# A hybrid RG-LRU and attention block: the stacked neighbour rows of the gate tiles copied by ScalarE and VectorE, and the first gate tile stacked as well

## The chip, the core and the metric

The kernel runs on one core of one Trainium2 chip. The metric is the device time of one execution in microseconds, the median of several runs. TensorE multiplies, VectorE, ScalarE and POOL (GpSimd) work element by element, SP (SyncE) issues transfers, and so can ScalarE's queue.

## What is computed

One layer of an encoder over 1024 frames of width 1024, in float32. Only its recurrent branch matters here:

```python
u = conv(u) + conv_b                                   # depthwise, 4 taps, 1280 channels
ub = u.reshape(B, S, N_LRU_BLOCKS, LRU_BLOCK)          # 16 blocks of 80 channels
r = jax.nn.sigmoid(jnp.einsum("bsnc,ncd->bsnd", ub, w_rg).reshape(B, S, D_RNN) + b_rg)
i = jax.nn.sigmoid(jnp.einsum("bsnc,ncd->bsnd", ub, w_ig).reshape(B, S, D_RNN) + b_ig)
log_a = -LRU_C * r.astype(jnp.float32) * jax.nn.softplus(-lru_lambda.astype(jnp.float32))
a = jnp.exp(log_a)
b = jnp.sqrt(-jnp.expm1(2.0 * log_a)) * (i * u).astype(jnp.float32)
_, h = lax.associative_scan(_lru_combine, (a, b), axis=1)
```

The rest (windowed attention, merge of the branches, SwiGLU) is large, and the change doesn't touch it.

## The kernel before

Frames are worked on in two halves of 512 (`h` = 0, 1); channels lie on the 128 partitions. Each float32 product is made of three matmuls over operands that are split in a high and a low part: high x high, high x low, low x high. Weights are loaded by SP into a ring of four blocks `w_raw` and split by POOL into `w_hi` and `w_lo`. A load is issued when the block that was in its place is split, and a block is split when TensorE is done with the one before it in its place (`blocks_done`).

**Gate tiles.** The 1280 channels make ten tiles of 128, `j` = 0 to 9, but the gates' blocks have 80 channels, so a tile's gates need its own channels and some of a neighbour tile. Of tiles 1, 2, 3, 6, 7, 8 (`MIXED`) the needed rows of both neighbours together fill one operand of 128 partitions, `mix_hi` and `mix_lo`, in slot `j % 3`. Tiles 4, 5 and 9 (`NEAR`) need only 32 rows of one neighbour. Theirs are stacked: partitions 0 to 31 of `mix_hi` hold the high part, 32 to 63 the low part, 64 to 95 the high part again, with weights stacked to match, and one matmul over 96 partitions does what three do elsewhere. Tile 0 needs 16 channels of tile 1; it reads tile 1's `uc_hi` and `uc_lo` whole, with three matmuls. So a gate has six matmuls in tiles 0 to 3 and 6 to 8, and four in tiles 4, 5 and 9; each tile has two gates (r and i).

**A step.** `recurrent` on TensorE runs steps `j` = 2 to 9. In each: `project(0)`, 24 matmuls, makes the conv's input of tile `j`; then `gates(j - 2)`, 12 or 8 matmuls; then `project(2)`, 24 matmuls, the GeLU branch. So in this text step 6 makes the gates of tile 4, step 7 those of tile 5, step 8 those of tile 6. The gates of tiles 8 and 9 follow in `kvq`.

ScalarE in step `j`, in this order: `conv_in` (L1369 to L1378, which waits for `project(0)`), the rounding of an output (L1435), the gates' functions of tile `j - 2` (tanh L1403 and L1405, exp L1410, tanh L1412, which wait for the gates), `conv_hi` (L1383: the high part `uc_hi` of tile `j`), `gate_root` (a table load and a sqrt, L1418), `mix` (the transfers L1390 and L1395, which wait for `uc_lo`), `decay` (L1430, waits for VectorE) and the GeLU (a table load and L1424). VectorE in step `j`: three taps of the conv (L1927), L1963, the low part `uc_lo` (L1933, behind `uc_hi`), and the recurrence of tile `j - 2` (L1939 to L1957).

**The transfers.** `mix(j)` copies, from partition to partition, rows of tile `j` into the operands of its neighbours `j - 1` and `j + 1`: one transfer of 256 KB into each mixed one (L1390), three of 64 KB into a stacked one (L1395). They are issued on ScalarE's queue. A mixed tile `j` is complete with the transfer from tile `j + 1`, in step `j + 1`, and its gates follow in step `j + 2`. TensorE waits for them in `gates`, ahead of the tile's first matmul; the trace gives that wait at L915.

## Time and profile before

| | |
|---|---|
| median of 3 runs | 1620.09 us |
| lowest, highest | 1619.33, 1626.31 us |
| profiled execution, device time | 1621.06 us |
| its span, first to last instruction | 1619.2 us |
| instructions | 24286 |
| granted TensorE clock, mean | 0.997 of full speed |
| VectorE busy | 905.0 us (56%) |
| ScalarE busy | 572.3 us (35%) |
| POOL busy | 1234.4 us (76%) |
| DMA | 188.86 MB, mean 117 GB/s |

Times of the profile count from the first instruction of the span. Busy time of TensorE overlaps (a matmul of 512 columns is shown with 0.39 us, and the next one starts 0.23 us behind its start), so its stream is read by starts. PE is TensorE's matmul, PEld its weight load, DVE VectorE, ACT ScalarE; a name with q is that engine's sequencer or queue. Brackets behind a row give the engine's idle time before it and what ended it.

### The profile page before, as it was taken

The numbers are of one execution on the slowest core, as the hardware profiler recorded it, in microseconds if no ns is written. First come the engines' busy times: TensorE is split into PE (matmuls) and PEld (weight loads), VectorE is DVE, ScalarE is ACT, GpSimd is POOL, SyncE is SP. The second block draws the span as 40 slices with busy tenths as digits, with TensorE's granted clock in tenths as the row PEclk, the third lists the DMA queues.
The fourth block names the chain that finished last, engine by engine and source line by source line (L and its number), as shares of the span: only waits on it lengthen the run. The fifth ranks groups of instructions, "written<-read, shape, count | busy, mean of one in ns | idle before, by whom it ended". The sixth has DMA issues, their size and how long they took to land.

```text
span 1619.2 us, 24286 instructions
## 1 busy us (share of the span) xinstructions
PE 1603.6 (99%) x7390; PEld 1327.0 (82%) x7390; DVE 905.0 (56%) x1158; ACT 572.3 (35%) x1078; POOL 1234.4 (76%) x1330
## 2 busy tenths in 40 slices
PE   9999999999999999999999999999999999999997
PEld 7888888888888888888888878888888888788887
DVE  6565646652165666676622579677865558405502
ACT  4787335532226885255422244100010013102100
POOL 5787866777777788777777777788887778877875
PEclk9999999999999999999999999999999999999999
DMA  5445432233344454522333583344422222733632
GB/s 165 131 120 131 132 91 80 74 101 93 97 144 128 121 133 114 166 77 74 92 97 95 150 286 107 97 118 117 119 75 75 65 65 69 245 93 114 222 107 87
DMA packets 121462, 188.86 MB, mean 117 GB/s; under 512 B 13668, under 2 KB 45796, under 8 KB 121380
## 3 DMA queue, kind: packets, MB, share of 16 engines
q1 hardware_dynamic: 97476, 144.03, 32.1%
q10 hardware_dynamic: 23904, 43.79, 8.2%
q8 instruction: 45, 0.74, 0.2%
q14 instruction: 37, 0.30, 0.1%
HBM read 162.73 MB, written 17.56 MB: 111 GB/s over the span
## 4 chain that ended last, share of the span: by engine, by line
PE 90%; DVE 4%; issue 2%; ACT 2%; ACTq 0%; DMA 0%; POOL 0%; DVEq 0%; SPq 0%; POOLq 0%
PE ps L872 14%; PE ps L871 14%; PE ps L870 14%; PE ps L1128 8%; PE ps L1127 8%; PE ps L1129 8%; PE ps L1225 4%; PE ps L1226 4%; PE ps L1227 4%; PE ps L950 1%; PE ps L946 1%; PE ps L947 1%; PE ps L1038 1%; DVE rows L2152 1%; DVE rows_r L2311 1%
## 5 line engine op out<-in xcount | busy, mean ns | idle before, releaser
L688 POOL TENSOR_TENSOR w_lo<-w_raw,w_hi 128x512 fp32r<-128x512 f32 (+2 forms) x374 | 448.3, 1199 | 31.2
L685 POOL TENSOR_SCALAR w_hi<-w_raw 128x512 fp32r<-128x512 f32 (+2 forms) x374 | 242.5, 648 | 194.4 <-PE ps L872 127.3
L872 PE MATMUL ps<-h_hi,w_lo 128*128 128x512 f32 x672 | 263.8, 393 | 0.0
L871 PE MATMUL ps<-h_lo,w_hi 128*128 128x512 f32 x672 | 263.6, 392 | 0.0
L870 PE MATMUL ps<-h_hi,w_hi 128*128 128x512 f32 x672 | 262.1, 390 | 0.7 <-DVE g_h L1950 0.6
L870 PEld LDWEIGHTS ps<-h_hi,w_hi 128*128 128x128 f32 x672 | 126.2, 188 | 28.9 <-DVE g_h L1950 1.5
L871 PEld LDWEIGHTS ps<-h_lo,w_hi 128*128 128x128 f32 x672 | 126.2, 188 | 27.5
L872 PEld LDWEIGHTS ps<-h_hi,w_lo 128*128 128x128 f32 x672 | 126.3, 188 | 26.1
L1127 PE MATMUL ps<-t,w_hi 128*128 128x512 f32 x352 | 138.2, 392 | 0.6 <-POOL w_lo L763 0.5
L1128 PE MATMUL ps<-t,w_hi 128*128 128x512 f32 x352 | 138.7, 394 | 0.0
L1129 PE MATMUL ps<-t,w_lo 128*128 128x512 f32 x352 | 136.6, 388 | 0.0
L1894 DVE TENSOR_TENSOR acc<-acc,sq 128x512 f32<-128x512 f32 x31 | 33.7, 1088 | 146.4 <-ACT sq L1620 134.2
L717 POOL TENSOR_SCALAR w_hi<-w_raw 128x512 fp32r<-128x512 f32 (+1 forms) x100 | 65.3, 653 | 45.5 <-PE ps L872 40.5
L730 POOL TENSOR_TENSOR w_lo<-w_raw,w_hi 128x512 fp32r<-128x512 f32 x72 | 93.8, 1303 | 6.0
L763 POOL TENSOR_TENSOR w_lo<-w_raw,w_hi 128x512 fp32r<-128x512 f32 x60 | 87.0, 1451 | 5.0
L1717 ACT ACTIVATE rstd_a<-rstd_a 128x512 f32<-128x512 f32 x22 | 13.9, 632 | 194.9 <-DVE rstd_a L2298 194.9
L1127 PEld LDWEIGHTS ps<-t,w_hi 128*128 128x128 f32 x352 | 66.1, 188 | 16.8 <-issue 1.4
L1129 PEld LDWEIGHTS ps<-t,w_lo 128*128 128x128 f32 x352 | 66.1, 188 | 14.8
L1128 PEld LDWEIGHTS ps<-t,w_hi 128*128 128x128 f32 x352 | 66.2, 188 | 13.1
L2119 DVE SCALAR_TENSOR_TENSOR tmp<-tmp,ps 128x512 f32<-128x512 f32 x16 | 11.0, 688 | 114.0 <-PE ps L872 114.0
L1620 ACT ACTIVATE sq<-ps 128x512 f32<-128x512 f32 (+1 forms) x15 | 9.0, 598 | 178.8 <-PE ps L1227 174.7
L1539 ACT ACTIVATE prob<-prob,stat 128x128 f32<-128x128 f32 x128 | 49.7, 389 | 63.3 <-DVE stat L2048 63.3
(389 smaller groups left out, 4105.7 us busy)
## 6 DMA issues: line engine op xcount, KB each, us to landing
w_raw<-w_f SPq DMA_DIRECT2D x68, 256.0 KB, 3.2
w_raw<-w_step SPq DMA_DIRECT2D x64, 256.0 KB, 2.8
w_raw<-w_b SPq DMA_DIRECT2D x64, 256.0 KB, 3.1
w_raw<-w_d SPq DMA_DIRECT2D x64, 256.0 KB, 2.7
w_raw<-w_a SPq DMA_DIRECT2D x96, 128.0 KB, 2.1
w_raw<-w_q SPq DMA_DIRECT2D x32, 256.0 KB, 3.1
w_raw<-w_o SPq DMA_DIRECT2D x32, 256.0 KB, 3.1
mix_hl<-uc_hl ACTq DMA_DIRECT2D x24, 256.0 KB, 4.7
```

Source lines behind the costliest of these rows:

```text
L685: nc.gpsimd.tensor_scalar(w_hi[:, s, w], w_raw[:, s, w], 1.0, 0.0, ALU.mult, ALU.add).then_inc(w_hi_made, 1)
L688: nc.gpsimd.tensor_tensor(w_lo[:, s, w], w_raw[:, s, w], rd(w_hi[:, s, w]), ALU.subtract).then_inc(w_lo_made, 1)
L717: nc.gpsimd.tensor_scalar(w_hi[:, s, w], w_raw[:, s, w], 1.0, 0.0, ALU.mult, ALU.add).then_inc(w_hi_made, 1)
L730: nc.gpsimd.tensor_tensor(w_lo[:, s, w], w_raw[:, s, w], rd(w_hi[:, s, w]), ALU.subtract).then_inc(w_lo_made, 1)
L763: nc.gpsimd.tensor_tensor(w_lo[:, s, :], src, rd(w_hi[:, s, :]), ALU.subtract)\
L870: mm(out, w_hi[:, s, w], x_hi, start=(k == 0), stop=False)
L871: mm(out, w_hi[:, s, w], x_lo, start=False, stop=False)
L872: last = mm(out, w_lo[:, s, w], x_hi, start=False, stop=(k == total - 1))
L1127: mm(ps[:, bank, :], w_hi[:, slot, w], x_hi[:, k, :], start=(q == 0), stop=False)
L1128: mm(ps[:, bank, :], w_hi[:, slot, w], x_lo[:, k, :], start=False, stop=False)
L1129: last = mm(ps[:, bank, :], w_lo[:, slot, w], x_hi[:, k, :], start=False, stop=(q == K2 - 1))
L1225: mm(out, w_hi[:, s, w], hi(k), start=(k == 0), stop=False)
```

## The change

The three transfers into each stacked tile go. Instead ScalarE, right behind `uc_hi` of the neighbour tile, copies 32 rows of it to partitions 0 to 31 and 64 to 95 of the operand, and VectorE, behind `uc_lo`, subtracts the same 32 rows (conv result less `uc_hi`) into partitions 32 to 63. These copies move data between partitions, for tile 4 from tile 3, for tile 5 from tile 6, for tile 9 from tile 8. Tile 0 joins the stacked tiles, with rows 0 to 31 of tile 1: its gates have four matmuls each in place of six, SP loads its weights with two transfers per block, one of which repeats 32 rows three times, and POOL splits them as for the other stacked tiles. TensorE waits on two new semaphores for the stacked tiles, and on `mix_made` for the mixed ones alone.

```diff
-NEAR = {4: (3, P - 32), 5: (6, 0), 9: (8, P - 32)}
-STACK = ((0, 0), (32, 1), (64, 0))
+NEAR = {0: (1, 0), 4: (3, P - 32), 5: (6, 0), 9: (8, P - 32)}
+NEAR_LIST = list(NEAR)
 STACKED = 96
 
 def mix_count(h, j):
-    same = range(j % 3, KR, 3)
-    dmas = [2 if i in MIXED else len(STACK) if i in NEAR else 0 for i in same]
-    return 16 * (h * sum(dmas) + sum(dmas[:j // 3 + 1]))
+    same = [i for i in MIXED if i % 3 == j % 3]
+    return 32 * (h * len(same) + same.index(j) + 1)
+
+def near_count(h, j):
+    return len(NEAR) * h + NEAR_LIST.index(j) + 1
...
+        def near_of(j):
+            return [(to, slice(r, r + 32)) for to, (of, r) in NEAR.items() if of == j]
...
-                    elif i not in NEAR:
-                        sp_eng.dma_start(w_raw[:, s, 0:2 * P], dram[g, :, off:off + 2 * P])\
-                            .then_inc(w_loaded[s], 16)
                     else:
-                        own = off + P
+                        own = off + (P if i else 0)
...
-                    if size < 4 and i:
+                    if size < 4:
                         used[s] += 2 if i in MIXED else 1
...
-                if j:
+                if j in MIXED:
                     pe.wait_ge(mix_made[j % 3], mix_count(h, j))
+                else:
+                    pe.wait_ge(near_hi_made, 2 * near_count(h, j))
+                    pe.wait_ge(near_lo_made, near_count(h, j))
...
                     if j not in NEAR:
-                        near_hi, near_lo = ((mix_hi[:, j % 3, :], mix_lo[:, j % 3, :]) if j else
-                                            (uc_hi[:, 1, :], uc_lo[:, 1, :]))
+                        near_hi, near_lo = mix_hi[:, j % 3, :], mix_lo[:, j % 3, :]
...
             def conv_hi(h, j, q):
                 act.wait_ge(taps, (j + KR * h) * 3 + 3)
                 fn(uc_hi[:, q, :], uc_of(q), ACT.Copy).then_inc(uc_hi_made, 1)
+                for to, r in near_of(j):
+                    act.wait_ge(uc_hi_made, j + KR * h + 1)
+                    for row in (0, 64):
+                        fn(mix_hi[row:row + 32, to % 3, :], rd(uc_hi[r, q, :]), ACT.Copy)\
+                            .then_inc(near_hi_made, 1)
...
-                    elif to in NEAR and NEAR[to][0] == j:
-                        r = slice(NEAR[to][1], NEAR[to][1] + 32)
-                        for row, part in STACK:
-                            act.dma_start(rd(mix_hi[row:row + 32, to % 3, :]), rd(uc_hl[r, part, j % 4, :]))\
-                                .then_inc(mix_made[to % 3], 16)
...
                 tt(uc_lo[:, q, :], uc_of(q), rd(uc_hi[:, q, :]), ALU.subtract)\
                     .then_inc(uc_lo_made, 1)
+                for to, r in near_of(j):
+                    tt(mix_hi[32:64, to % 3, :], uc_of(q)[r, :], rd(uc_hi[r, q, :]), ALU.subtract)\
+                        .then_inc(near_lo_made, 1)
```

## Rows read from the trace of the kernel before

**Rows 1.** Part 1 of the page: busy time, share of the span, number of instructions.

```profile
PE 1603.6 (99%) x7390; PEld 1327.0 (82%) x7390; DVE 905.0 (56%) x1158; ACT 572.3 (35%) x1078; POOL 1234.4 (76%) x1330
```

**Rows 2.** Timeline of TensorE, tiles 0, 5, 1 (second half): start, length, instruction.

```profile
45.14 0.39 PE L917 MATMUL ps<-uc_hl,w_hi 128*128 128x512 f32 x1
...
47.89 0.39 PE L870 MATMUL ps<-h_hi,w_hi 128*128 128x512 f32 x1
...
112.93 0.39 PE L917 MATMUL ps<-uc_hl,w_hi 128*128 128x512 f32 x1
...
114.78 0.40 PE L870 MATMUL ps<-h_hi,w_hi 128*128 128x512 f32 x1
...
518.73 0.39 PE L917 MATMUL ps<-uc_hl,w_hi 128*128 128x512 f32 x1
```

**Rows 3.** Timeline of TensorE at the start of tile 6's gates.

```profile
125.55 0.40 PE L872 MATMUL ps<-h_hi,w_lo 128*128 128x512 f32 x1
...
125.97 0.47 PE L917 MATMUL ps<-uc_hl,w_hi 128*128 128x512 f32 x1
...
126.28 0.40 PE L918 MATMUL ps<-uc_hl,w_hi 128*128 128x512 f32 x1
```

**Rows 4.** TensorE's waits at L915 (length in ns): tiles 6, 1 (second half), 2.

```profile
L915 PEldq EVENT_SEMAPHORE  x1: 4231/4231/4231, 121.7 to 121.7; - x1
...
L915 PEldq EVENT_SEMAPHORE  x1: 3316/3316/3316, 514.6 to 514.6; - x1
...
L915 PEldq EVENT_SEMAPHORE  x1: 3764/3764/3764, 68.5 to 68.5; - x1
```

**Rows 5.** Timeline of ScalarE in steps 6 and 7.

```profile
106.42 0.57 ACT L1383 ACTIVATE uc_hl<-ps 128x512 fp32r<-128x512 f32 x1
...
110.64 0.63 ACT L1430 ACTIVATE g_a<-g_r 128x512 f32<-128x512 f32 x1 [1.70 <-DVE g_s L1943]
...
112.58 0.60 ACT L1424 ACTIVATE gy<-ps 128x512 f32<-128x512 f32 x1
...
113.23 0.20 ACT L1369 ACTIVATE u_raw<-u_carry 128x3 f32<-128x3 f32 x1
...
114.76 0.62 ACT L1435 ACTIVATE lru_hi<-g_h 128x512 fp32r<-128x512 f32 x1
...
115.29 0.67 ACT L1403 ACTIVATE g_r<-ps,half_b 128x512 f32<-128x512 f32 x1
...
120.60 0.65 ACTq L1390 DMA_DIRECT2D mix_hl<-uc_hl  x1
```

**Rows 6.** Timeline of ScalarE in step 4.

```profile
72.91 0.20 ACT L1369 ACTIVATE u_raw<-u_carry 128x3 f32<-128x3 f32 x1 [0.39 <-PE ps L872]
...
75.64 0.69 ACT L1403 ACTIVATE g_r<-ps,half_b 128x512 f32<-128x512 f32 x1 [0.58 <-PE ps L925]
```

**Rows 7.** Timeline of POOL, ScalarE and VectorE around tile 0, first and second half.

```profile
39.97 0.41 POOL L717 TENSOR_SCALAR w_hi<-w_raw 128x256 fp32r<-128x256 f32 x1 [1.52 <-PE ps L950]
...
41.58 0.60 ACT L1383 ACTIVATE uc_hl<-ps 128x512 fp32r<-128x512 f32 x1 [2.49 <-DVE ps L1927]
...
510.56 2.25 DVE L1927 SCALAR_TENSOR_TENSOR ps<-u_raw,par,ps 128x512 f32<-128x512 f32 x3
```

**Rows 8.** Timeline of VectorE in step 6.

```profile
109.05 0.69 DVE L1942 SCALAR_TENSOR_TENSOR g_r<-g_a,g_r 128x512 f32<-128x512 f32 x1 [0.73 <-ACT g_s L1418]
...
109.66 0.95 DVE L1943 SCALAR_TENSOR_TENSOR g_s<-g_a,g_s 128x512 f32<-128x512 f32 x1
```

**Rows 9.** Instructions of L1933 and L1943: count, ns min/median/max.

```profile
L1933 DVE TENSOR_TENSOR uc_hl<-ps,uc_hl x20: 691/692/693, 34.2 to 607.4; 128x512 fp32r<-128x512 f32 x20
...
L1943 DVE SCALAR_TENSOR_TENSOR g_s<-g_a,g_s x20: 677/680/1784, 55.8 to 636.8; 128x512 f32<-128x512 f32 x20
```

**Rows 10.** Instructions of L1544 and L1539 between 244 and 245 us.

```profile
L1544 ACTq FUSED_REGOPS  x1: 43/43/43, 244.6 to 244.6; - x1
...
L1539 ACT ACTIVATE prob<-prob,stat x4: 385/386/387, 243.8 to 245.0; 128x128 f32<-128x128 f32 x4
```

More of the change, by code:

```diff
@@ L399, in build @@
             sem("a_made"), sem("gelu_made"), sem("lru_hi_made"))
+        near_hi_made, near_lo_made = sem("near_hi_made"), sem("near_lo_made")
         iu_made, loss_made, amp_made, b_made, scanned, h_kept, lru_made, lru_lo_made = (
@@ L545, in load_gates @@
                                          .rearrange("(o r) c -> o r c", o=1)
-                                         .broadcast_to([len(STACK), 32, P])).then_inc(mix_loaded[s], 16)
+                                         .broadcast_to([STACKED // 32, 32, P])).then_inc(mix_loaded[s], 16)
                         sp_eng.dma_start(w_raw[:, s, 0:P], dram[g, :, own:own + P])\
```

## The prediction

> **What bounds the kernel now.** Part 1 of the page comes first: TensorE's matmuls are busy for 99% of the span [rows 1]. So time can only be had by giving TensorE less to do or by closing a gap in its stream, and it can only be lost by opening one. The change touches the gate tiles, so I next read TensorE's timeline there. A tile with three near-matmuls per gate takes from 45.14 to 47.89, 2.75 us for twelve matmuls; a stacked tile takes from 112.93 to 114.78, 1.85 us for eight [rows 2]. Both run at one pace, 0.23 us from start to start.
>
> The third view is TensorE's own wait ahead of a gate tile. The wait for the transfers that fill `mix_hl` ended at 121.7 + 4.23 = 125.9 for tile 6, and the first matmul began at 125.97, 0.42 us behind the one before it, and the next 0.31 us later [rows 3, 4]. Against the pace of 0.23 that is (0.42 - 0.23) + (0.31 - 0.23) = 0.27 us lost. So the transfers of the mixed tiles land just in time, and the list of idle times, which sees hardly any of this because matmul records overlap, would not have told it. Who is late at tile 6? ScalarE's timeline answers: from 113.23, right behind the gelu that ends at 113.18, it works without a pause to the gates' tanh at 115.29, on to the exps and the copy `uc_hi`, and the transfer for tile 6 goes out at 120.60 [rows 5]. In the steps of full-length gates ScalarE does pause for TensorE: 0.39 us ahead of L1369, 0.58 us ahead of L1403 [rows 6]. Tile 6 is different since the gates of tile 5 ahead of it are the short, stacked ones: TensorE is through them 0.9 us sooner, ScalarE isn't.
>
> **The change part by part.**
>
> *Tile 0 stacked.* Two halves, each 2.75 - 1.85 = 0.90 us: 1.80 us off TensorE, if nothing is late next. Its stacked rows come from tile 1. In the first half the copy `uc_hi` of tile 1 starts at 41.58, two ScalarE copies follow and are through by about 43.4, and the gates start at 45.14: free [rows 2, 7]. POOL makes a tile-0 block by four short instructions in place of two; it had waited 1.52 us for TensorE ahead of this block and has made it by some 41.2, over 4 us before use: free [rows 7]. SP issues four loads for the two blocks in place of two; POOL's releaser there is TensorE, not a load: free. If that cover were gone each would cost its own length, about 0.5 us.
>
> *What is late next at tile 1.* With tile 0 shorter, TensorE reaches tile 1 0.90 us sooner. In the first half the transfer for tile 1 hangs on ScalarE's chain behind the gates of tile 0, so it moves along. In the second half it doesn't: the conv of tile 2 starts at 510.56 only, behind VectorE's reciprocal, which nothing here moves [rows 7]. TensorE's wait ended at 514.6 + 3.32 = 517.92 [rows 4]. The matmul was at 518.73 [rows 2]; it would come at 517.83. By tile 6, a matmul follows the end of its wait by 0.06 us and loses 0.08 more behind it: 517.92 + 0.14 - 517.83 = 0.23 us lost.
>
> *Transfers of tiles 4, 5, 9 removed.* 18 issues of some 0.6 us on ScalarE's queue and 18 transfers go. Nobody waited for them: those of tiles 4 and 9 are done a step before use, those of tile 5 in time. The ScalarE instruction behind them (L1430) waits for VectorE's L1943 anyway [rows 5]. Worth nothing; at most a loss of tile 6's kind, 0.27 us, goes at tile 7, should its transfer land sooner with none behind it.
>
> *Sixteen ScalarE copies of 32x512.* Rows of such a copy don't exist; a copy takes by its columns, so I take the 128x512 copy L1435: 0.62 us, and the next starts 0.52 us behind its start [rows 5]. The first must wait for the copy `uc_hi` to end. In step 6 (for tile 5): L1383 ends at 106.99, copy one 107.05, copy two 107.57 to 108.19. What stood right behind L1383 stands behind copy two: ScalarE is 108.19 - 106.99 = 1.20 us later. VectorE's L1942 waits for the sqrt behind it and moves by as much, from 109.05 to 110.25, and L1943 from 109.66 to 110.86 [rows 8]. L1943 took 0.95 us here and 0.68 us at its median [rows 9], so L1430 starts at 111.57 to 111.84 in place of 110.64. The gelu ends at 114.11 to 114.38 in place of 113.18. L1369 followed TensorE at 113.23, so it is now 0.85 to 1.12 us later, and from there to the transfer for tile 6 nothing is slack. Tile 6 already waits, so all of it is new wait: 2 x (0.85 to 1.12) = 1.70 to 2.24, middle 1.97 us. The copies for tiles 4 and 9 (steps 3 and 8) delay ScalarE as much, but the next step holds 0.39 + 0.58 us of pauses [rows 6] before it could reach the transfers for tiles 3 and 8: nothing. The lower bound is zero in step 7 too, if the 32-row copies were far shorter than any row; the upper is the delay in every step (a rival).
>
> *Do the copies hold back the transfer issued behind them?* In steps 3 and 8 the transfers for tiles 2 and 7, due at once, stand behind the new copies in ScalarE's program. They start when `uc_lo` is made, if the sequencer runs ahead of the engine. It does: at 244.60 the sequencer handles L1544, which stands behind nine exps in the program, while the engine begins the fourth [rows 10]. So the transfers still go out on time: nothing.
>
> *Eight VectorE subtractions* of 32x512, PSUM and SBUF in. The row alike is L1933: 0.691 to 0.693 us in all 20 [rows 9]. VectorE waits for the sqrt there (0.73 us idle ahead of L1942 [rows 8]) and has the time: nothing. The trace also shows L1943, two SBUF inputs, at 0.68 to 1.78 us [rows 9]. The Trainium skill ("SBUF — State Buffer", Who interferes with whom) has it that a VectorE instruction with two SBUF inputs is blocked by a GpSimd one that reads SBUF, and blocks it in turn. By that rule the new subtraction, one input from PSUM, stays at 0.69 us, and the trace's constant L1933 agrees; but L1942 and L1943 of step 6, moved by 1.2 us, may fall on another POOL instruction and take up to 1.1 us more or lose the 0.27 they now have too much, which would put tile 6 at 0.85 to 2.2 us per half.
>
> **Sum.** -1.80 + 0.23 + 1.97 = +0.40 us. The profiled execution took 1621.06 us (span 1619.2, 1.9 around it), which gives 1621.46; the median of the runs stands 0.97 below it: 1620.09 + 0.40 = 1620.5. Its own range is the sum's ends (+0.13 to +0.67) and half a microsecond per half for how long the tile 6 transfer takes when it starts later: 1619.3 to 1621.8.
>
> **The rivals.**
> (a) *The delay never reaches tile 6*, because the copies are short or the pauses take it up. Then -1.80 + 0.23 = -1.57: 1618.5. For it: ScalarE's queue loses 18 issues of 0.6 us. Against: those issues lie beside the engine's work, and the path from 113.18 on is closed. 0.27.
> (b) *Slower: the transfers for tiles 2 and 7 wait behind the copies.* Each goes out up to 1.2 us later. Tile 2's wait ended at 68.5 + 3.76 = 72.3 [rows 4]; its first matmul came at about 72.6, by L1369 at 72.91, which the matmul before it (0.39 us long) released [rows 6]. Less the 0.14 us from wait to matmul that is about 0.2 us of room. Priced for all four with that room: 4 x (1.2 - 0.2) = 4.0 us on the forecast, 1624.5. It decides from the point where the issue starts over 0.1 us behind the end of `uc_lo`. Against: [rows 10]. 0.10.
> (c) *The delay passes through steps 4 and 9 as well*, to tiles 3 and 8: four times 1 us, less their room, for which tile 2's 0.2 us stands: 3.2 us on the forecast, 1623.7. Against: the pauses [rows 6]. 0.08.
> (d) *The change doesn't do its work*: tile 0 is not shorter, since a stacked matmul contracts over fewer rows and not fewer columns. The timeline of tile 5 excludes it: same pace, fewer matmuls. 0.02.
>
> **How the numbers follow.** The forecast has 0.51, (a) 0.27, (b) 0.10, (c) 0.08, (d) and the rest 0.04. The range of 8 in 10 takes in the forecast, (a) with some tenths for the spread of the runs, and (c): 1618.2 to 1623.8. It leaves out (b) and the rest. A measurement of this kernel can tell about 0.5%, 8.1 us, from no change. No case reaches that; even 1.2 us in each of eight places comes to 9.6 - 1.8 = 7.8. So same 0.97, faster 0.01 and slower 0.02, for what isn't thought of.
>
> **What would show it.** Tile 0: from its first matmul to the next projection's 1.85 us, like tile 5, with eight matmuls. Tile 6: the two matmul intervals at its start sum to 1.1 to 1.4 us over pace in both halves, and ScalarE's tanh of tile 5's gates about 1 us later against TensorE. Tile 1 of the second half: 0.2 us over pace. L1390 in steps 3 and 8 still at the end of `uc_lo`; the table load in steps 3, 6 and 8 about 1.2 us behind the end of `uc_hi`. If tile 6 is no later than before, (a) holds and I took the copies too long or the path too tight; if L1390 starts late in steps 3 and 8, (b). The prediction is most exposed in the length of one transfer (5.3 us for tile 6) and in where VectorE meets POOL.

## The result, and the profile after

The changed kernel took 1624.3 us (median of 12; the kernel before 1620.8 us, median of 12 beside it). The ratio is 1.0023, with a 95% interval of 1.0015 to 1.003: the change costs 3.5 us by the medians and 0.23% by the ratio. That is less than the 0.5% below which the prediction calls two times the same, but the interval doesn't hold 1. One of the twelve executions took 1988.41 us at a granted clock of 0.752 and is left out of the ratio. The forecast was +0.4 us, 1620.5 us, and the time lies above the top of the range, 1623.8. The profiled execution took 1625.44 us with a span of 1623.6 us, 4.4 above that of before (1619.2), at a mean granted clock of 0.996.

Part 1 of the page after, beside [rows 1]: TensorE has eight matmuls fewer and is as busy as before, VectorE is 16 us busier (of which the eight subtractions are 5.5) and ScalarE 9.

```profile
PE 1603.8 (99%) x7382; PEld 1326.6 (82%) x7382; DVE 920.9 (57%) x1166; ACT 581.1 (36%) x1094; POOL 1239.7 (76%) x1338
```

What TensorE waited for, by line (total us, times, longest us); L925 is the first matmul of a gate tile, as L917 was before.

```profile
PE ps L925 <- issue: 3.9, 4, 1.3
...
PE ps L1045 <- DVE prob L2066: 1.3, 2, 1.0
...
PE ps L875 <- ACT gy L1431: 0.4, 1, 0.4
```

Four gate tiles wait now. The timeline of TensorE says which, and what has become of tile 0: tile 0 (first half, first matmul, and the next projection's), tile 6 (first half), tile 1 (second half), a projection in step 4 (second half), tile 3 (second half), and tile 6 (second half).

```profile
45.40 0.39 PE L925 MATMUL ps<-uc_hl,w_hi 128*128 128x512 f32 x1
...
47.26 0.40 PE L875 MATMUL ps<-h_hi,w_hi 128*128 128x512 f32 x1
...
126.72 0.47 PE L925 MATMUL ps<-uc_hl,w_hi 128*128 128x512 f32 x1 [1.32 <-issue]
127.03 0.39 PE L926 MATMUL ps<-uc_hl,w_hi 128*128 128x512 f32 x1
...
519.76 0.47 PE L925 MATMUL ps<-uc_hl,w_hi 128*128 128x512 f32 x1 [0.61 <-issue]
520.07 0.40 PE L926 MATMUL ps<-uc_hl,w_hi 128*128 128x512 f32 x1
...
536.10 0.39 PE L932 MATMUL ps<-mix_hl,w_lo 128*128 128x512 f32 x1
536.94 0.51 PE L875 MATMUL ps<-h_hi,w_hi 128*128 128x512 f32 x1 [0.45 <-ACT gy L1431]
...
549.00 0.47 PE L925 MATMUL ps<-uc_hl,w_hi 128*128 128x512 f32 x1 [0.78 <-issue]
549.31 0.40 PE L926 MATMUL ps<-uc_hl,w_hi 128*128 128x512 f32 x1
...
590.21 0.47 PE L925 MATMUL ps<-uc_hl,w_hi 128*128 128x512 f32 x1 [1.23 <-issue]
```

Tile 0 takes 47.26 - 45.40 = 1.86 us in place of 2.75, as forecast. The losses are counted as in the prediction, by the starts against a pace of 0.23 us; the profile's bracket is smaller than a start interval, since records overlap. Tile 6 loses 1.57 us in the first half (its first matmul starts 1.71 behind the one before it, the next 0.31 later) and 1.48 in the second, where it lost 0.27 and 0.33 before [rows 3]. Tile 1 of the second half loses 0.85, tile 3 of the second half 1.03, and the projection of step 4 in the second half 0.72 (intervals 0.84 and 0.34). Tile 7, which lost 0.15 before in the first half, loses nothing.

From the first matmul of tile 0 to that of tile 9, the two halves took 116.78 + 116.69 us before and 117.11 + 119.87 after: +3.51 us. This is the whole of the measured 3.5 to 3.7. The single entries make

| us, after less before | |
|---|---|
| tile 0, both halves | -1.80 |
| tile 1, second half | +0.85 |
| tile 6, 1.30 + 1.15 | +2.45 |
| step 4, second half: projection 0.72, tile 3 1.03 | +1.75 |
| tile 7 | -0.15 |
| sum | +3.10 |

and 0.4 us are left. Of these, 0.25 lie behind tile 3 of the second half: from 549.31 to 563.08 us TensorE's matmuls start 0.2333 us apart, and elsewhere in these steps 0.2289, at a granted clock of 1.00 in both. The rest of the span's 4.4 is a later start (0.26) and a wait of 0.52 at the start of the first half's attention (747 ns at 250.02, L1045), which the kernels below have or don't have without a pattern that could be tied to the change.

Now to ScalarE in steps 6 and 7, beside [rows 5].

```profile
105.84 0.57 ACT L1390 ACTIVATE uc_hl<-ps 128x512 fp32r<-128x512 f32 x1
106.44 1.29 ACT L1394 ACTIVATE mix_hl<-uc_hl 32x512 fp32r<-32x512 f32 x2
107.17 0.60 ACTq L1402 DMA_DIRECT2D mix_hl<-uc_hl  x1
107.75 1.28 ACT L1425 ACT_TABLE_LOAD   x1
...
111.53 0.63 ACT L1437 ACTIVATE g_a<-g_r 128x512 f32<-128x512 f32 x1 [1.85 <-DVE g_s L1953]
...
113.48 0.60 ACT L1431 ACTIVATE gy<-ps 128x512 f32<-128x512 f32 x1
...
116.02 0.67 ACT L1410 ACTIVATE g_r<-ps,half_b 128x512 f32<-128x512 f32 x1
...
121.33 0.61 ACTq L1402 DMA_DIRECT2D mix_hl<-uc_hl  x1
```

The copies (L1394) hold the engine from 106.41 to 107.75, 1.34 us, where 1.20 was forecast. `decay` (L1437) starts 5.12 us behind the end of `uc_hi` (106.41 to 111.53); before it was 110.64 - 106.99 = 3.65 [rows 5]. Of these 1.47 us, 1.32 come from the copies (L1952 below starts 3.38 us behind `uc_hi`, L1942 stood 2.06 behind it), and 0.15 is VectorE's, whose L1953 took 1.10 us and not 0.95 [rows 8]. From there to the transfer for tile 6 there are 121.33 - 111.53 = 9.80 us, before 9.96 [rows 5]: a closed path, as foreseen. ScalarE's tanh of tile 5's gates comes 3.67 us behind their first matmul (112.34 to 116.02), 2.36 before [rows 2, 5]: 1.3 us later, where about 1 was forecast. The third row is the one that bears on rival (b): the transfer for tile 7 goes out at 107.17, in the middle of the copies.

VectorE and POOL in the same step:

```profile
109.79 0.69 DVE L1952 SCALAR_TENSOR_TENSOR g_r<-g_a,g_r 128x512 f32<-128x512 f32 x1 [1.34 <-ACT g_s L1425]
110.40 1.10 DVE L1953 SCALAR_TENSOR_TENSOR g_s<-g_a,g_s 128x512 f32<-128x512 f32 x1
```

```profile
109.92 1.04 POOL L722 TENSOR_SCALAR w_hi<-w_raw 128x512 fp32r<-128x512 f32 x1 [0.33 <-PE ps L877]
```

And in step 3 of the second half, VectorE, then POOL, then ScalarE:

```profile
531.87 1.84 DVE L1952 SCALAR_TENSOR_TENSOR g_r<-g_a,g_r 128x512 f32<-128x512 f32 x1 [1.18 <-ACT g_s L1425]
```

```profile
531.86 1.29 POOL L735 TENSOR_TENSOR w_lo<-w_raw,w_hi 128x512 fp32r<-128x512 f32 x1
```

```profile
534.34 0.64 ACT L1437 ACTIVATE g_a<-g_r 128x512 f32<-128x512 f32 x1 [2.57 <-DVE g_s L1953]
...
536.29 0.60 ACT L1431 ACTIVATE gy<-ps 128x512 f32<-128x512 f32 x1
```

This is a row that the sum had no term for. VectorE's L1952, two SBUF inputs and 0.69 us long in most steps, starts 0.01 us behind POOL's L735 and takes 1.84 us. `decay` starts at 534.34, the GeLU ends at 536.89, the projection of step 4 starts at 536.94 on its release, and ScalarE, which begins step 4 this late, has no pause left before the transfer for tile 3.

The step was late before it came to its copies. In step 2 of the second half VectorE's two instructions take 1.09 and 1.78 us:

```profile
516.64 1.09 DVE L1952 SCALAR_TENSOR_TENSOR g_r<-g_a,g_r 128x512 f32<-128x512 f32 x1 [0.73 <-ACT g_s L1425]
517.65 1.78 DVE L1953 SCALAR_TENSOR_TENSOR g_s<-g_a,g_s 128x512 f32<-128x512 f32 x1
```

So step 3 begins late: `uc_lo` of tile 3 is made 529.24 - 519.76 = 9.48 us behind the first matmul of tile 1's gates, in the first half 8.37, and 8.35 in the kernel before. These 1.13 us come on top of the copies.

The three lines that the steps of the prediction spoke of (count, ns min/median/max):

```profile
L1394 ACT ACTIVATE mix_hl<-uc_hl x16: 627/630/637, 42.3 to 598.6; 32x512 fp32r<-32x512 f32 x16
```

```profile
L1943 DVE TENSOR_TENSOR mix_hl<-ps,uc_hl x8: 680/687/694, 43.0 to 598.7; 32x512 fp32r<-32x512 f32 x8
```

```profile
L1953 DVE SCALAR_TENSOR_TENSOR g_s<-g_a,g_s x20: 678/1099/1785, 54.8 to 641.1; 128x512 f32<-128x512 f32 x20
```

L1953 is the L1943 of before [rows 9]; its median went from 680 to 1099 ns. The new subtraction, one input in PSUM, is never stretched (694 ns at most).

### The profile page after: what moved, and what is told of

The parts are those of the page before. It is cut to its first block, busy times and chain, and to the rows that moved or that the text cites. A ratio compares the mean times of both kernels' runs of the same rounds, so it can differ in the third digit from the quotient of the medians.

```text
span 1623.6 us, 24296 instructions
## 1 busy us (share of the span) xinstructions
PE 1603.8 (99%) x7382; PEld 1326.6 (82%) x7382; DVE 920.9 (57%) x1166; ACT 581.1 (36%) x1094; POOL 1239.7 (76%) x1338
## 4 chain that ended last, share of the span: by engine, by line
PE 88%; DVE 5%; issue 3%; ACT 3%; DMA 1%; ACTq 0%; POOL 0%; DVEq 0%; SPq 0%; POOLq 0%
PE ps L877 14%; PE ps L876 14%; PE ps L875 13%; PE ps L1134 8%; PE ps L1136 8%; PE ps L1135 8%; PE ps L1232 4%; PE ps L1233 4%; PE ps L1234 4%; PE ps L953 1%; PE ps L957 1%; PE ps L954 1%; PE ps L1045 1%; DVE rows L2162 1%; DVE rows_r L2321 1%
## 5 line engine op out<-in xcount | busy, mean ns | idle before, releaser
L735 POOL TENSOR_TENSOR w_lo<-w_raw,w_hi 128x512 fp32r<-128x512 f32 x72 | 99.0, 1374 | 6.0
L768 POOL TENSOR_TENSOR w_lo<-w_raw,w_hi 128x512 fp32r<-128x512 f32 x60 | 87.1, 1451 | 5.0
```

The lines of the kernel that those rows point to most:

```text
L735: nc.gpsimd.tensor_tensor(w_lo[:, s, w], w_raw[:, s, w], rd(w_hi[:, s, w]), ALU.subtract).then_inc(w_lo_made, 1)
L768: nc.gpsimd.tensor_tensor(w_lo[:, s, :], src, rd(w_hi[:, s, :]), ALU.subtract)\
```

## The experiments

The theory: the copies make ScalarE late by their own length ahead of `decay`, in steps 6 and 3; at tile 6 this is lost at once, and in step 3 it is lost only where VectorE meets POOL as well. The rivals: the loss comes from tile 0's change and what it shifts; or it is mostly the meeting of VectorE and POOL, and the copies' length matters little. Ratios are against the kernel before on the same chip, with 95% intervals.

### The two halves of the change alone

`e1_tile0_only`: tile 0 stacked by copies, tiles 4, 5 and 9 by transfers as before.

```diff
-NEAR_LIST = list(NEAR)
+NEAR_LIST = [0]
+STACK = ((0, 0), (32, 1), (64, 0))
...
+                    elif to in NEAR and to not in NEAR_LIST and NEAR[to][0] == j:
+                        r = slice(NEAR[to][1], NEAR[to][1] + 32)
+                        for row, part in STACK:
+                            act.dma_start(rd(mix_hi[row:row + 32, to % 3, :]), rd(uc_hl[r, part, j % 4, :]))\
+                                .then_inc(mix_made[to % 3], 16)
```

> Tile 0 stacked by two ScalarE copies and one VectorE subtraction; tiles 4, 5 and 9 by transfers, as in the kernel before. My theory (the loss is ScalarE's delay by the copies in steps 3 and 6): tile 0 gives 2 x 0.90 = 1.80 us, tile 1 of the second half loses 0.85 us as in the changed kernel, tile 6 loses its old 0.3 us and no more, so 0.9 to 1.0 us faster than before, about 1619.8. Rival (a shorter tile 0 alone shifts the engines against each other and costs elsewhere): tile 3 of the second half or tile 6 lose a microsecond here too, and the time is equal to before or slower.

Measured: 1619.96 us, ratio 0.9996 (0.9984 to 1.0008). Tile 6 loses nothing in either half (its transfers took 4.92 and 4.91 us), tile 1 of the second half 0.86 us, tile 3 of the second half 0.10.

`e2_no_tile0`: tiles 4, 5 and 9 by copies, tile 0 as before.

```diff
-NEAR = {0: (1, 0), 4: (3, P - 32), 5: (6, 0), 9: (8, P - 32)}
+NEAR = {4: (3, P - 32), 5: (6, 0), 9: (8, P - 32)}
```

> Tiles 4, 5 and 9 by copies, tile 0 as before, unstacked. My theory: tile 6 loses 1.5 us in place of 0.3 in both halves (+2.4), tile 7 loses nothing in place of 0.15, so at least 2.2 us slower than before, about 1623.0; with the second half's VectorE wait in step 3 as well (+1.75), 1624.8. Rival (tile 0's change is the cause): no more than 0.5 us slower.

Measured: 1623.28 us, ratio 1.0016 (1.0005 to 1.0028). Tile 6 loses 1.78 and 1.23 us, no other tile anything. So the loss at tile 6 belongs to the copies, that at tile 1 of the second half to tile 0's stack. The two parts don't add up: by the medians -0.93 and +2.39 us against 1620.89 make +1.5, and both together cost 3.5. The entries of the traces say where the rest is: 1.75 us are those of step 4 in the second half, of which `e1_tile0_only` has 0.10 and `e2_no_tile0` nothing; and `e1_tile0_only` gains the 0.60 us that tile 6 lost before, which the whole change doesn't. (The traces' sums are -1.58 and +2.99; 0.68 of the latter is no wait but the slower pace of 0.2333 us, from 127 to 163 us.) Step 3 of `e2_no_tile0` in the second half says why. Two rows of VectorE in step 2, then one of VectorE and one of POOL in step 3:

```profile
516.66 0.69 DVE L1956 SCALAR_TENSOR_TENSOR g_r<-g_a,g_r 128x512 f32<-128x512 f32 x1 [0.73 <-ACT g_s L1429]
517.27 0.69 DVE L1957 SCALAR_TENSOR_TENSOR g_s<-g_a,g_s 128x512 f32<-128x512 f32 x1
```

```profile
530.88 0.69 DVE L1956 SCALAR_TENSOR_TENSOR g_r<-g_a,g_r 128x512 f32<-128x512 f32 x1 [1.18 <-ACT g_s L1429]
```

```profile
531.21 0.84 POOL L725 TENSOR_SCALAR w_hi<-w_raw 128x512 fp32r<-128x512 f32 x1 [1.50 <-PE ps L880]
```

Two things differ from the changed kernel. In step 2 nothing is stretched, and `uc_lo` of tile 3 is made 8.35 us behind the first matmul of tile 1, not 9.48. In step 3 the copies are there and L1956 is as late behind them, but it starts 0.33 us ahead of a POOL instruction and not just behind one; with L1957 the pair takes 1.79 us (0.69 and 1.10) and not 2.52 (1.84 and 0.68). The GeLU of step 3 ends 15.27 us behind the first matmul of tile 1, in the changed kernel 17.13: of these 1.86 us, 1.13 are brought along from step 2 and 0.73 arise in step 3. `e1_tile0_only` has the stretched step 2 as well (1.09 and 1.78 us, `uc_lo` at 9.48) but no copies in step 3, and loses 0.10. With tile 0 shorter, TensorE's stream, and with it POOL's, stands otherwise against VectorE's, in step 2 already. No run separates the 1.13 from the 0.73 beside the copies.

### The copies moved within the step

Copies can stand further back in ScalarE's program, behind the sqrt and the transfers, where ScalarE waits for VectorE anyway (1.85 us ahead of `decay` in the rows above). `e3_copies_late` does this in steps 3, 6 and 8.

```diff
+LATE = (3, 6, 8)
...
+                if j not in LATE:
+                    near_copies(h, j, q)
...
+                    if j in LATE:
+                        near_copies(h, j, j % 4)
```

> The changed kernel with ScalarE's copies of steps 3, 6 and 8 put behind the sqrt and the transfers, into ScalarE's idle time ahead of L1437; nothing else moved, VectorE's subtractions included. My theory: ScalarE's sqrt comes 1.3 us sooner again, tile 6 loses 0.3 us as in the kernel before, tile 3 of the second half nothing, tile 1 of the second half still 0.85 us: -1.80 + 0.85 = 0.95 us faster than before, about 1619.8. Rival (VectorE's eight subtractions, or transfers that land later because of what else changed, cost the time): tile 6 still loses 1 us or more and the time stays within 1 us of the changed kernel's 1624.3.

Measured: 1620.02 us, ratio 0.9992 (0.9981 to 1.0004); `e10_late_again` below, the same kernel, gives 1620.07. ScalarE in step 6, and TensorE at tile 6:

```profile
104.89 0.57 ACT L1391 ACTIVATE uc_hl<-ps 128x512 fp32r<-128x512 f32 x1
...
106.78 0.63 ACT L1430 ACTIVATE g_s<-g_r 128x512 f32<-128x512 f32 x1
107.31 1.27 ACT L1399 ACTIVATE mix_hl<-uc_hl 32x512 fp32r<-32x512 f32 x2
109.13 0.63 ACT L1442 ACTIVATE g_a<-g_r 128x512 f32<-128x512 f32 x1 [0.54 <-DVE g_s L1960]
```

```profile
124.00 0.39 PE L878 MATMUL ps<-h_hi,w_lo 128*128 128x512 f32 x1
124.23 0.39 PE L926 MATMUL ps<-uc_hl,w_hi 128*128 128x512 f32 x1
```

The same two copies stand in a pause of which 0.54 us is still left, `decay` starts 109.13 - 105.46 = 3.67 us behind `uc_hi` as before the change, and tile 6 starts in pace. The only loss of size is tile 1 of the second half, 1.18 us.

Three kernels move part of this. `e4_step6_late` has `LATE = (6,)`, `e5_step3_late` has `LATE = (3,)`, and `e7_one_copy` has step 6 alone and moves one of its two copies:

```diff
-                    for row in (0, 64):
+                    for row in rows:
...
+                near_copies(h, j, q, (0,) if j in LATE else (0, 64))
...
+                    if j in LATE:
+                        near_copies(h, j, j % 4, (64,))
```

> As the run with all copies put behind the sqrt, but only those of step 6 (for tile 5); steps 3 and 8 stay as in the changed kernel. My theory: tile 6's extra loss goes (2.4 us), the loss of step 3 in the second half (tile 3 and the projection ahead of it, 1.75 us) stays: about 1621.9. Rival (the delay of step 3 is what reaches tile 6): tile 6 still loses over 1 us and the time is above 1623.

> The changed kernel with ScalarE's copies of step 3 alone (for tile 4) put behind the sqrt; those of steps 6 and 8 stay ahead of it. My theory (two separate losses): the loss in the second half at the projection of step 4 and at tile 3 (0.7 + 1.0 us) goes, the loss at tile 6 (1.5 us in each half) stays: about 1622.5. Rival (one lag that begins in step 3 and is passed on to tile 6): tile 6 loses under 0.6 us too, and the time is about 1620.

> The changed kernel with one of step 6's two copies put behind the sqrt, the other left ahead of it: half the delay. My theory (tile 6 waits for all that ScalarE is late): tile 6 loses 0.85 to 1.0 us in place of 1.5 in each half, about 1623.1. Rival (the loss comes by a collision of VectorE and POOL that either occurs or doesn't): tile 6 loses either 0.3 or 1.5 us.

Measured (losses in us over pace, ' for the second half):

| | median us | ratio, interval | tile 6, 6' | tile 1' | step 4', tile 3' |
|---|---|---|---|---|---|
| changed kernel | 1624.3 | 1.0023, 1.0015 to 1.003 | 1.57, 1.48 | 0.85 | 0.72, 1.03 |
| step 3 late | 1622.49 | 1.0013, 1.0004 to 1.0022 | 0.97, 1.35 | 0.98 | none |
| one copy of step 6 late | 1622.22 | 1.0011, 1.0002 to 1.002 | 0.19, 0.70 | 1.06 | 0.48, 0.74 |
| step 6 late | 1621.26 | 1.0005, 0.9994 to 1.0016 | none, 0.27 | 0.96 | 0.57, 0.69 |
| steps 3, 6, 8 late | 1620.02 | 0.9992, 0.9981 to 1.0004 | none | 1.18 | none |

The copies lose time in two separate places: those of step 6 at tile 6, and those of step 3 at step 4 and tile 3. `e5_step3_late` came out as expected, `e4_step6_late` 0.6 us sooner, `e7_one_copy` 0.9 us sooner than its 1623.1.

The loss at tile 6 has two terms, and only one is the copies'. In the eight halves with both copies ahead of `decay` (the changed kernel, `e2`, `e5`, `e8` below) the transfer goes out 8.99 to 9.01 us behind the first matmul of tile 5, and the loss is its length less 3.7 us: 4.70 us long, it loses 0.97; 5.30 long, 1.57; 5.50 long, 1.78. In the kernel before it goes out at 7.68, and 5.28 us of length lose 0.27. So the copies are worth 1.3 us per half at equal length, and the spread of the length as much as 0.8.

The one copy left ahead of `decay` in `e7_one_copy` made the tanh of tile 5's gates 0.52 us late in the first half and 1.16 in the second. The difference is VectorE's and POOL's order. In the first half both start at 109.41, VectorE's L1958 1 ns behind POOL's L710, and POOL's is the one that is stretched (1.01 us, VectorE 0.69). In the second half VectorE is 10 ns behind POOL, and it is VectorE's:

```profile
571.02 1.00 DVE L1958 SCALAR_TENSOR_TENSOR g_r<-g_a,g_r 128x512 f32<-128x512 f32 x1 [0.68 <-ACT g_s L1429]
```

```profile
571.01 0.46 POOL L710 TENSOR_TENSOR w_lo<-w_raw,w_hi 128x128 fp32r<-128x128 f32 x1
```

So neither expectation of `e7_one_copy` held alone: half the copies and a meeting that occurs or doesn't both count.

In the kernel with step 6 late, tile 7 of the first half lost 0.62 us in turn: its transfer took 5.80 us, in the changed kernel 3.16. In that kernel step 3 is as in the changed one, and VectorE and POOL meet once more, this time at the second of the two instructions:

```profile
531.27 1.79 DVE L1960 SCALAR_TENSOR_TENSOR g_s<-g_a,g_s 128x512 f32<-128x512 f32 x1
```

```profile
530.76 1.74 POOL L736 TENSOR_TENSOR w_lo<-w_raw,w_hi 128x512 fp32r<-128x512 f32 x1
```

### Is it the copies or the meeting with POOL?

`m2_after_memset` is the changed kernel with POOL's splits of the weights that take 128x512 in the recurrent stage, and in the stages ahead and behind, replaced by memsets, which read nothing: the products with those weights are left out. `m1_before_memset` is the same in the kernel before.

```diff
-                        nc.gpsimd.tensor_scalar(w_hi[:, s, w], w_raw[:, s, w], 1.0, 0.0,
-                                                ALU.mult, ALU.add).then_inc(w_hi_made, 1)
+                        if size == 4:
+                            nc.gpsimd.memset(rd(w_hi[:, s, 0:2 * P]), 0.0)
+                            nc.gpsimd.memset(rd(w_hi[:, s, 2 * P:4 * P]), 0.0).then_inc(w_hi_made, 1)
...
+                        for part in range(8):
+                            last = nc.gpsimd.memset(rd(w_lo[:, s, 64 * part:64 * part + 64]), 0.0)
```

> The kernel before, with POOL's two instructions for each 128x512 weight block of the head, step and tail stages replaced by memsets of about the same length (two of 256 columns, eight of 64), which write and don't read; so these weights are zero and the projections of these stages leave their products out. Loads, waits and order stay. My theory (VectorE's instructions with two SBUF inputs wait for a POOL instruction that reads SBUF): in steps 2 to 9 no L1942 or L1943 takes over 0.75 us, other than beside the 128x256 and stacked blocks that stay; the time is within 1 us of the kernel before. Rival (the stretched lengths have to do with when VectorE starts against ScalarE): they stay stretched beside the memsets.

> The changed kernel with the same memsets in POOL, and the same products left out. My theory: VectorE's L1952 at 1.84 us and L1953 at 1.10 us in the steps with copies go back to 0.69 us; the second half's loss of 1.7 us behind step 3 goes or falls to under 0.5 us, tile 6 still loses by the copies alone, 1.0 to 1.3 us in each half. So against the same kernel without the change 0.5 to 1.5 us slower in place of 3.5. Rival (the collisions are a by-product, the copies alone do it all): tile 3 of the second half still loses 1 us and the difference stays 3 us or more.

Measured: 1619.63 us, ratio 0.9993 (0.9984 to 1.0001), for the kernel before, whose gate tiles lose nothing more (0.05 us in all); 1619.46, ratio 0.9989 (0.998 to 0.9997), for the changed one, which loses only 0.65 us at tile 1 of the second half and nothing at tile 6. One row of VectorE in step 6 of the latter, and the transfers of its mixed tiles (the last line gives the time to landing):

```profile
109.81 0.68 DVE L1958 SCALAR_TENSOR_TENSOR g_s<-g_a,g_s 128x512 f32<-128x512 f32 x1
```

```profile
L1407 ACTq DMA_DIRECT2D mix_hl<-uc_hl x24: 597/603/693, 34.6 to 606.6; - x24
...
DMA to landing us min/median/max: 3.1/3.3/5.0
```

`m1_before_memset` came out as expected. `m2_after_memset` didn't: at tile 6, 1.0 to 1.3 us of loss were expected in each half, and 0.5 to 1.5 us of time over `m1_before_memset`. But the run does two things at once, and its time is no proof of either side. The stretch is gone in step 6: the tanh of tile 5's gates came 3.26 us behind their first matmul, in the changed kernel 3.67 and before 2.36. So the copies alone make ScalarE 0.90 us late here and the meeting with POOL adds 0.41. But the memsets are also shorter than the splits (0.76 us for the second in place of 1.30), the loads go out earlier, and the transfer for tile 6 landed in 3.67 us where it took 5.30 in the changed kernel and 5.28 before. It landed 0.59 us ahead of tile 6's first matmul, so tile 6 would have been in time even with the 0.41. In the second half the stretch of step 2 is gone too (0.69 and 0.68 us), `uc_lo` of tile 3 is made at 8.43 and not 9.48, and tile 3 loses nothing. What the pair shows is the share of the meeting in the delay, and that tile 6 hangs on its transfer's length as much as on ScalarE.

### What stands behind tile 1 of the second half

Its transfer waits for the conv of tile 2, which waits for VectorE. Ahead of that conv VectorE sets a sum (`open_sum`) and four blocks of `kd` to zero. `e6_late_memsets` is `e3_copies_late` with all five memsets behind `uc_lo` of tile 2, `e8_after_memsets` the same in the changed kernel, and `e9_best` is `e3_copies_late` with the four of `kd` alone, at the end of the recurrent stage; `e10_late_again` is `e3_copies_late` once more, as its partner.

The edit of `e6_late_memsets`:

```diff
-                open_sum(1 + 2 * h)
-
-                for kd in (kd_hi, kd_lo):
-                    for half in range(2):
-                        r = slice(64 * half, 64 * half + 64)
-                        nc.vector.memset(rd(kd[r, :, 1 - half, :]), 0.0).then_inc(kd_zeroed, 1)
...
+                    if j == 2:
+                        open_sum(1 + 2 * h)
+                        for kd in (kd_hi, kd_lo):
+                            ...
```

> All ScalarE copies of steps 3, 6, 8 behind the sqrt, and VectorE's memsets behind tile 2's low part: both known losses taken away. My theory: total loss at the gate tiles under 0.5 us, so nearly the whole 1.80 us of tile 0 and the 0.8 us that the kernel before loses at its gates: 1.5 to 2.3 us faster than before, about 1619.0. Rival (the gain is capped by something behind the gates, as the end of the recurrence or the attention): the gates lose nothing, and still no faster than the 1620.0 of the kernel with late copies alone.

> The changed kernel, with VectorE's memsets (1.8 us) moved from ahead of tile 2's conv to behind its low part, nothing else. My theory (tile 1 of the second half waits since the conv of tile 2 is late there, and its step's lateness starts the loss of step 3): the transfer for tile 1 goes out at least 0.4 us sooner, tile 1 loses 0 to 0.45 us in place of 0.85, and the second half's loss behind step 3 (1.75 us) goes or shrinks, since without tile 0's change it did not occur: about 1621.7 to 1622.5. Rival (tile 3's loss comes from step 3's copies alone): only tile 1's part goes, about 1623.5.

> The kernel with ScalarE's late copies, and VectorE's four memsets of the key tiles moved from ahead of tile 2's conv to the end of the recurrent stage; the memset of the sum stays. My theory: the conv of tile 2 starts 1.3 us sooner, tile 1 of the second half loses under 0.5 us in place of 1.2; if the last attention chunk isn't hit by the collision that cost the kernel with all memsets late 1.4 us, 1.3 to 2.0 us faster than before, about 1619. Rival (tile 1's loss is the transfer's length, not its start): it still loses 0.8 us or more, and the time equals the one with late copies alone.

> The kernel with late copies once more, for a narrower interval: 0.5 to 1.3 us faster than before by the trace's sum (gates 1.3 us shorter, first attention chunk 0.5 us longer). Rival (no gain at all; the first measurement was luck): ratio 1.0000 or above.

Measured: `e6` 1620.46 us (0.9996, 0.9986 to 1.0006), `e8` 1625.62 (1.0032, 1.002 to 1.0044), `e9` 1618.74 (0.9994, 0.9981 to 1.0006), `e10` 1620.07 (0.9994, 0.9985 to 1.0004). In all three kernels with the memsets moved, the loss at tile 1 of the second half is gone: its transfer goes out 7.35 us (`e6`, `e8`) and 7.80 us (`e9`) behind the first matmul of tile 0 and not 9.20. So that wait was VectorE's. Yet only `e9` has a lower median than its like without the move, and the interval of its ratio holds 1. `e6` missed its 1619.0, and `e8` missed its 1621.7 to 1622.5 by over 3 us: it was expected that the loss behind step 3 of the second half would go or shrink with the one at tile 1, and tile 3 still loses 1.03 us. In `e8` tile 3 of the first half, in time in the changed kernel, loses 0.91 us as well. In both halves step 3 begins 0.48 us late (`uc_lo` at 8.83, since VectorE's step 2 has the memsets in it), and VectorE's two instructions then take 1.00 or 1.01 and 1.78 us beside the copies: the same three terms as in the changed kernel, each of another size.

The stages behind the first attention of the second half took 6.7 us more in the profiled execution of `e8` than in the changed kernel's (930.4 against 923.7). A wait of 1.26 us for VectorE at 808.39 is part of it. The rest is no wait. The same stretch of both, first `e8`, then the changed kernel (window, its length, then busy us and number of instructions of PE, PEld, DVE, ACT and POOL; granted clock, share and GB/s of the DMA):

```profile
1055.00:1350.00 295.00, 294.52 (x1262) 238.27 (x1262) 188.43 (x236) 29.65 (x48) 235.43 (x216) 1.00 0.31 87
```

```profile
1055.00:1350.00 295.00, 294.53 (x1287) 241.36 (x1286) 196.95 (x243) 29.66 (x48) 240.28 (x219) 1.00 0.32 87
```

TensorE is busy for all but 0.5 us in both, but `e8` gets through 25 matmuls fewer: they start 0.2333 us apart and not 0.2289, some 5.5 us in all, at a granted clock of 1.00 in both. No line of the edit acts there, and this execution took 1630.23 us, 4.6 above the median of its kernel. So it is taken here for this execution's, not the edit's; what sets the pace isn't known. Why the median of `e8` stands above the changed kernel's isn't shown: its gate stages are 0.90 us shorter, and the wait at 808.39 takes that back.

In `e6` the gate tiles lose 0.50 us in all, less than in `e3` (1.30), and the time isn't shorter. VectorE and POOL in the last attention stage, first `e6`, then `e3`:

```profile
801.50 1.75 DVE L2088 TENSOR_TENSOR q_lo<-rstd_a,q_hi 128x512 fp32r<-128x512 f32 x1 [1.30 <-ACT q_hi L1574]
```

```profile
801.41 1.30 POOL L694 TENSOR_TENSOR w_lo<-w_raw,w_hi 128x512 fp32r<-128x512 f32 x1
```

```profile
801.05 0.73 DVE L2088 TENSOR_TENSOR q_lo<-rstd_a,q_hi 128x512 fp32r<-128x512 f32 x1 [0.92 <-ACT q_hi L1574]
```

```profile
801.33 1.61 POOL L694 TENSOR_TENSOR w_lo<-w_raw,w_hi 128x512 fp32r<-128x512 f32 x1
```

In `e6` VectorE starts 0.09 us behind POOL and takes 1.75 us; TensorE then waits for it (1.29 us at 804.56). In `e3` VectorE starts 0.28 us ahead, takes 0.73, POOL's instruction takes 1.61 in place of 1.30, and TensorE doesn't wait there. What was won in one stage is given back in another by the order of two instructions 0.3 us apart.

## Why the prediction was wrong

*Tile 0, -1.80.* Right: 1.86 us per tile, and nothing of POOL's, SP's or ScalarE's added work ahead of it is late (`e1_tile0_only`).

*Tile 1 of the second half, +0.23; it was +0.85.* The mechanism was right, the size wrong. The issue stands where it was foreseen: 9.20 us behind the first matmul of tile 0 (506.14 to 515.34), before 9.21. But the step took the transfer's 3.7 us over from the trace of before, and it took 4.33. Before, the load that SP issues stood at 514.84, behind the transfer at 514.20; now it stands at 515.10, ahead of the transfer at 515.34. Counted from tile 0's first matmul the load goes out at 8.96 us and not 9.85: TensorE, 0.9 us earlier, frees the weight block earlier. The two halves of the change agree: 4.33 us in `e1_tile0_only`, with a load 0.24 ahead, 3.67 in `e2_no_tile0`, with one 0.65 behind.

*Tile 6, +1.97; it was +2.45.* The path is the one described, and this wait is the largest entry. Two terms were mis-sized, and ScalarE is 1.3 us late where 0.85 to 1.12 was forecast (114.11 and 114.38 less 113.23, the prediction's own figures, are 0.88 and 1.15). The copies were priced by a 128x512 copy that overlaps the next by 0.10 us; they are as long (0.63) but leave a gap of 0.03, so two hold the engine for 1.34 us and not 1.20. And L1953 was to take between 0.68 and 0.95 us; it took 1.10. The transfer's length, the third term, happened to be nearly the same as before (5.30 and 5.19 us against 5.28 and 5.33); that was luck, as the 4.70 to 5.50 us of the other kernels show. The sentence on the meeting with POOL had allowed for this, up to 2.2 us a half, but the sum and the range's ends took in only the gentle half of it.

*The copies of steps 3 and 8, nothing; they cost +1.75.* This is the step that failed: the pauses of 0.39 + 0.58 us [rows 6] were to take up the whole delay. They don't, not even where nothing is lost. Here is ScalarE at the start of step 4 of the first half, where 0.39 us of idle time stood before:

```profile
73.45 0.20 ACT L1376 ACTIVATE u_raw<-u_carry 128x3 f32<-128x3 f32 x1
```

The pause ahead of L1410 is gone as well, and the transfers for tiles 3 and 8 go out 8.85 us behind the first matmul of the tile ahead, before 8.37 to 8.46. So 0.4 to 0.5 us get through, as rival (c) had it, and cost nothing because these transfers had 0.33 to 0.74 us of room before and have 0.34 to 0.79 now. In the second half of the changed kernel this cover isn't enough, since two more delays come to the copies' 1.34 us: 1.13 from VectorE's meeting with POOL in step 2, which goes back to tile 0's change, and 0.73 more of VectorE in step 3 than in `e2_no_tile0`. Rival (c) described the path, priced at 3.2 us for four places; the loss came in one. The prediction reasoned on the two VectorE instructions in step 6 alone, where a row of the trace had shown L1943 at 1.78 us somewhere [rows 9], and it took tile 0's part and the copies' part as independent.

The Trainium skill ("SBUF — State Buffer", Who interferes with whom) has it that a VectorE instruction with two SBUF inputs contends with a GpSimd one that reads SBUF, not with one that only writes it, and that "Issue order, not op shape, decides who blocks." The traces agree: L1952 stretched to 1.84 us by a POOL instruction of 1.29 us that started 0.01 us ahead of it, POOL's L694 stretched from 1.30 to 1.61 us where VectorE was ahead, 0.68 us for L1958 beside memsets, and 680 to 694 ns for the subtraction with its input in PSUM.

*Rival (b), transfers held back by the copies in ScalarE's program:* it didn't happen. L1402 goes out at 107.17 and at 529.27, 0.03 us behind the end of `uc_lo`, while the second copy runs. *Rival (a):* not in the changed kernel, but `e3_copies_late` is just that: 1620.02 against the 1618.5 that was given to it; what (a) missed is the 1.0 us more at tile 1 of the second half (a transfer of 4.65 us), and the rest lies within the interval. *Rival (d)* is refuted by 1.86 us.

*Transfers of tiles 4, 5 and 9: nothing.* Nearly so. Tile 7 gains its 0.15 us, and its transfer, with no three behind it, lands in 3.16 us where it took 5.34.

*The sum.* The terms missed are +0.62, +0.48 and +1.75, less 0.15 at tile 7: with the forecast's +0.40 they make the +3.10 of the table. By themselves they would not have left the range: 1620.5 + 2.7 is 1623.2, and the top stood 3.3 us above the forecast for rival (c). That the time lies 0.5 us above the top is in part the reference, whose median was 1620.09 us over three executions when the range was made and 1620.8 over twelve beside the result. The miss that counts is +3.5 us where +0.4 was forecast. All three errors are to one side, and the range was built from one case at a time, without a case in which the meeting with POOL, the copies' pitch and the transfer's length all go against the kernel.

What stays open: how long a transfer of a mixed tile flies (3.1 to 5.8 us in the changed kernel) is seen to go with loads and transfers beside it, but no run changed the loads alone. The meeting with POOL wasn't tried apart from POOL's own length, nor the one of step 2 apart from the one of step 3. Why TensorE's matmuls start 0.2333 us apart in some stretches isn't known. And whether the kernels with late copies are faster than the one before is not resolved: `e3_copies_late` and `e10_late_again` give 0.9992 and 0.9994, each with an interval that reaches past 1.

## What to carry to other kernels

An engine that produces just in time has idle gaps of its own; put added work into the gap whose end waits for another engine (here 1.85 us ahead of `decay`), not ahead of the instruction that this other engine waits for. The same copies, placed some 1.8 us later in the step, made the difference between +3.5 us and none that can be measured. Ask also whether the step is already late when the added work begins: a pause that takes up one delay doesn't take up two, and two edits that are harmless or cheap alone (`e1_tile0_only`, `e2_no_tile0`) cost 1.75 us more together. Where a delay moves VectorE instructions with two SBUF inputs, list every place where they come near a POOL instruction that reads SBUF, in each repetition of the step, and price each at up to 1.2 us: the repetitions don't behave alike. And of a transfer that lands just in time, its length is no constant of the trace: look at which loads go out around it and whether they move too.

## What the runs showed of the hardware that was not expected

ScalarE's copies of 32x512 from one set of 32 partitions to another take 0.63 us each (627 to 637 ns, 16 of them), as long as 128x512, but where 128x512 ones start 0.52 us behind each other, these stand 0.03 us apart: a pair costs 1.34 us, not 1.20.

A difference of 0.01 to 0.3 us in the order of a VectorE and a POOL instruction is worth up to 1.1 us to VectorE (L1952, L2088) or 0.3 us to POOL (L694), and the effect of a small edit in one stage can show in another, hundreds of us later (L2088 at 801.50).

A transfer of 256 KB between partitions landed in 3.1 to 5.8 us within one execution, and the same one in 3.71 or 4.33 us with a load issued 0.64 us behind it or 0.24 us ahead of it.

TensorE's 512-column matmuls start 0.2289 us apart in most of every trace and 0.2333 in some stretches (549 to 563 us in the changed kernel, 127 to 163 in `e2_no_tile0`, 1057 to 1349 in `e8_after_memsets`), without a pause and at a granted clock of 1.00 on both sides. Over the 292 us of the last that is 5.5 us, more than all that the change costs.
